# A static pipeline over heads in the gated-linear-attention stage

## The reference

```
cum = cumsum(log_a, within a chunk);  last = cum at the chunk's end
q_dec = q * exp(cum);  k_inv = k * exp(-cum);  k_end = k * exp(last - cum)
scores = tril(q_dec @ k_inv^T);  o_intra = scores @ v
upd = k_end^T @ v
S_next = exp(last) * S + upd;  o_inter = q_dec @ S
o = o_forward + flip(o_backward)
o = (o - mean(o)) * rsqrt(var(o) + 1e-5) * norm_g * silu(r)
```

## Time and profile before

| what | us |
|---|---|
| median of 3 runs (lowest, highest) | 3304.21 (3303.9, 3307.21) |
| the profiled execution's time | 3304.4 |
| its span, first to last instruction | 3302.6 |
| GLA stage, 528.4 to 1183.8 | 655.4 |
| of it PE busy, by the profile | 559.5 |
| one head | 157.2 |

### The profile page before, as it was taken

The page is one execution under the profiler, slowest core; times in us unless marked ns, Lnnn a source line. Parts: engine busy times, 40 slices in busy tenths (PEclk is TensorE's granted clock), DMA queues, the critical chain, the costliest instruction groups (busy, mean ns, idle before and its releaser), DMA issues. The chain is left out here.

```text
span 3302.6 us, 44198 instructions
## 1 busy us (share of the span) xinstructions
PE 2954.8 (89%) x17520; PEld 2849.0 (86%) x17520; DVE 1938.0 (59%) x2187; ACT 974.3 (29%) x1513; POOL 965.5 (29%) x458
## 2 busy tenths in 40 slices
PE   7999995979797959799996989999759999999993
PEld 7999995968686859799986989999649999999993
DVE  6666774253535376799996421455585555554556
ACT  2777774222313131244444110011240011100112
POOL 1121212111211012444541333434124333343430
PEclk9999997989898979899998999999879999999996
DMA  5132221010101033434334342322111111111111
GB/s 223 61 112 85 91 73 68 15 51 16 49 16 43 3 90 121 169 115 129 111 111 149 113 146 98 139 95 95 35 39 45 38 44 38 44 38 44 40 37 57
DMA packets 108091, 254.91 MB, mean 77 GB/s; under 512 B 20368, under 2 KB 51088, under 8 KB 107856
## 3 DMA queue, kind: packets, MB, share of 16 engines
q1 hardware_dynamic: 98192, 213.36, 19.4%
q10 hardware_dynamic: 9792, 40.11, 3.3%
HBM read 195.86 MB, written 57.55 MB: 77 GB/s over the span
## 5 line engine op out<-in xcount | busy, mean ns | idle before, releaser
L2063 PE MATMUL bank<-yhi,mrg_hi 128*128 128x384 f32 x1056 | 354.9, 336 | 34.3 <-POOL mrg_lo L167 20.6
L2063 PE MATMUL bank<-ylo,mrg_hi 128*128 128x384 f32 x1056 | 353.4, 335 | 0.0
L2063 PE MATMUL bank<-yhi,mrg_lo 128*128 128x384 f32 x1056 | 353.4, 335 | 0.0
L1417 PE MATMUL bank<-hhi,s_hi 128*128 128x384 f32 x768 | 265.6, 346 | 33.8 <-POOL s_lo L180 30.6
L164 POOL TENSOR_TENSOR mlp_hi<-mlp_raw,zero 128x1024 fp32r<-128x1024 f32 x64 | 121.9, 1905 | 534.5 <-PE bank L2390 225.9
L2390 PE MATMUL bank<-ahi,mlp_hi 128*128 128x384 f32 x768 | 257.4, 335 | 3.5 <-DVE alo L2439 3.5
L1417 PE MATMUL bank<-hhi,s_lo 128*128 128x384 f32 x768 | 259.4, 338 | 0.0
L1417 PE MATMUL bank<-hlo,s_hi 128*128 128x384 f32 x768 | 259.0, 337 | 0.0
L2390 PE MATMUL bank<-ahi,mlp_lo 128*128 128x384 f32 x768 | 256.6, 334 | 0.0
L2390 PE MATMUL bank<-alo,mlp_hi 128*128 128x384 f32 x768 | 256.5, 334 | 0.0
L2408 ACT ACTIVATE rl<-bank 128x384 f32<-128x384 f32 x96 | 47.0, 490 | 646.9 <-PE bank L2367 429.8
(11 more groups left out here) (396 smaller groups left out, 7758.4 us busy)
## 6 DMA issues: line engine op xcount, KB each, us to landing
mlp_raw<-in_mlp_units SPq DMA_DIRECT2D x64, 512.0 KB, 3.2
ada<-in_w_ada SPq DMA_DIRECT2D x32, 512.0 KB, 3.3
s_raw<-in_s_units SPq DMA_DIRECT2D x32, 512.0 KB, 4.3
mid_gates<-gate ACTq DMA_DIRECT2D x24, 576.0 KB, 3.5
gt<-mid_gates SPq DMA_DIRECT2D x24, 576.0 KB, 3.7
gla_raw<-in_gla_units SPq DMA_DIRECT2D x25, 512.0 KB, 3.6
lru_raw<-in_lru_units SPq DMA_DIRECT2D x24, 512.0 KB, 6.6
mid_s_tab<-tabq SPq DMA_DIRECT2D x8, 1152.0 KB, 7.6
```

The lines of the kernel that those rows point to most:

```text
L1417: mm = pe.matmul(out, wts[par][:, w], r[:, k, cols], start=(k == 0 and x == 0), stop=(k == KD - 1 and x == 2))
L2063: mm = pe.matmul(out, wt[par][:, w], r[:, slot, cols], start=(k == 0 and n == 0), stop=(k == len(order) - 1 and n == 2))
```

## The change

The `Fori` over heads is unrolled into a fixed order. While head h is in its 18 scan steps, PE also does one projection band in each step (v, q, k of head h+1 and r of head h-1, one band between scores(s+1) and outputs(s)) and small pieces of work called items: gates of this and the next head, transposes of the keys (three per item) and the mean and variance matmuls of head h-1. DVE and ACT get the matching work in the same step. Bands use banks 0 and 1, items banks 6 and 7, the scan banks 2 to 5, two for each step parity: scores with one update, and the other update with the output. `o` is doubled. r is no longer kept: each band goes to a buffer of 384 columns and is multiplied in at once. The root and the reciprocal are replaced by Ln and Exp with scale -0.5 on ACT. The high part of the weight split moves from POOL to ACT. On the host side only the order of the units in `gla_units` changes.

```diff
+        def step_band(h, s):
+            at = s if h else (s if s < 12 else None)
+            if h + 1 == HEADS:
+                at = s - 12 if s >= 12 else None
+            return [] if at is None else [HEAD_BANDS[h][at]]
+        def step_items(h, s):
+            got = []
+            if s == 0:
+                got.append(("gate", h, 1, 2))
+            if h and 1 <= s <= NB:
+                got.append(("mean", h - 1, 0, s - 1))
+            if h and 4 <= s < 4 + NB:
+                got.append(("var", h - 1, 0, s - 4))
+            if 7 <= s < 7 + NB:
+                got.append(("key", h, 1, s - 7))
+            if h + 1 < HEADS:
+                if s == 9:
+                    got += [("gate", h + 1, 0, 0), ("gate", h + 1, 0, 1)]
+                if s == 10:
+                    got.append(("gate", h + 1, 0, 2))
+                if s >= 15:
+                    got.append(("key", h + 1, 0, s - 15))
+            return got
+        def turn_items(h):
+            return [("value", h, 0, x) for x in range(NVT)] + [("gate", h, 1, 0), ("gate", h, 1, 1)]
...
-            return core.bank[3 * (s % 2) + 1 - c][:, P:P + DV]
+        def scores_psum(s):
+            return core.bank[2 + 2 * (s % 2)][:, 0:P]
+        def update_psum(s, c):
+            return core.bank[2 + 2 * (s % 2)][:, P:P + DV] if c else core.bank[3 + 2 * (s % 2)][:, 0:DV]
+        def out_psum(s):
+            return core.bank[3 + 2 * (s % 2)][:, DV:2 * DV]
...
+                def scores(h, s):                                   # PE
+                    g = NSTEP * h + s
+                    if g >= 2:
+                        pe.wait_ge(st_done, g - 1)
+                        pe.wait_ge(o_done, g - 1)
...
+                for h in range(HEADS):
+                    pe.wait_ge(band_free, 5 * NB if h == 0 else HEAD_BANDS[h - 1][2 * NB])
+                    for key in turn_items(h):
+                        item(key)
+                    scores(h, 0)
+                    for s in range(NSTEP):
+                        if s + 1 < NSTEP:
+                            scores(h, s + 1)
+                        for n in step_band(h, s):
+                            band(n)
+                        for key in step_items(h, s):
+                            item(key)
+                        outputs(h, s)
+                for x in range(NB):
+                    band(TAIL_BANDS[x])
+                    item(TAIL_MEANS[x])
+                band(TAIL_BANDS[NB])
+                for x in range(NB):
+                    item(TAIL_VARS[x])
+                for x in (4, 5):
+                    band(TAIL_BANDS[x])
...
+                    elif kind == "var":                             # ACT
+                        if NB * h + x:
+                            act.wait_ge(gm_done, NB * h + x)
+                        st(act.activation(scale[:], src[:, 0:BW], ACT.Ln, bias=eps[:, 0:1]))
+                        act.sem_inc(free_act, 1)
+                        act.activation(scale[:], scale[:], ACT.Exp, scale=-0.5).then_inc(rs_done, 1)
...
+                for h in range(HEADS):                              # DVE
+                    for s in range(NSTEP):
+                        advance(h, s)
                         if s:
-                            collect(s - 1)
+                            collect(h, s - 1)
+                        elif h:
+                            collect(h - 1, NSTEP - 1)
+                        if h >= 2 and s == 0:
+                            resonate(h - 2, 2 * NB - 1)
+                        if h and s <= NB:
+                            if s:
+                                centre(h - 1, s - 1)
+                            if s < NB:
+                                total(h - 1, s)
+                        if s == 5:
+                            keys(h, 1)
+                            queries(h, 1)
+                        if h and NB <= s < 2 * NB:
+                            spread(h - 1, s - NB)
+                        if h and 4 <= s < 4 + NB:
+                            normalise(h - 1, s - 4)
+                        if s == 2:
+                            forget(h, 1)
+                        if s == 3:
+                            accumulate(h, 1)
+                        if s == 6:
+                            ended(h, 1, 0)
+                            ended(h, 1, 1)
+                        if s == 7:
+                            ended(h, 1, 2)
...
+                        if h and s > 12:
+                            resonate(h - 1, s - 13)
```

More of the change, by code:

```diff
@@ L788, in start_state, with item_bank @@
+        counts = [0, 0]
+        for key in order + TAIL_MEANS + TAIL_VARS:
+            on_dve = key[0] == "mean"
+            ITEM[key] = len(FREED)
+            counts[on_dve] += 1
+            FREED.append((on_dve, counts[on_dve]))
+        def item_bank(key):
+            return core.bank[6 + ITEM[key] % 2]
         def start_state(s, c):
@@ L816, in _ @@
                 sync.dma_start(params[:], dram["gla_params"]).then_inc(small_in, 16)
+                load(1)
                 sync.dma_start(keep[:], dram["keep"]).then_inc(small_in, 16)
                 sync.dma_start(ident[:], dram["ident"]).then_inc(small_in, 16)
[L819 to L834, removed]
@@ L838, in _ @@
+                store_y(HEADS - 2)
+                store_y(HEADS - 1)
+                sync.wait_ge(y_out, 16 * HEADS)
                 for d in range(2):
-                    sync.wait_ge(final_out[d], 16 * HEADS + 16)
+                    sync.wait_ge(final_out[d], 16 * HEADS)
             @block.gpsimd
@@ L847, in _ @@
                         pool.memset(probs[d][s][:], 0.0).then_inc(const_done, 1)
[L848 to L852, removed]
+                for u in range(len(UNITS)):
+                    S.split_lo(pool, u, u % 2)
             @block.tensor
             def _(pe):
-                pe.wait_ge(const_done, 6)
@@ new lines, in band @@
+                def band(n):
+                    u, b = divmod(n, NB)
+                    if b == 0:
+                        pe.wait_ge(S.split_done, u + 3)
+                    if n >= 2:
+                        pe.wait_ge(band_free, n - 1)
+                    out = core.bank[n % 2][:, 0:BW]
+                    cols = slice(b * BW, (b + 1) * BW)
+                    for kk in range(KD):
+                        w = slice(kk * P, (kk + 1) * P)
+                        for x, (wts, r) in enumerate(((S.hi, hhi), (S.hi, hlo), (S.lo, hhi))):
+                            mm = pe.matmul(out, wts[u % 2][:, w], r[:, kk, cols],
+                                           start=(kk == 0 and x == 0), stop=(kk == KD - 1 and x == 2))
+                    mm.then_inc(band_mm, 1)
@@ L1106 @@
+                collect(HEADS - 1, NSTEP - 1)
+                resonate(HEADS - 2, 2 * NB - 1)
+                m = HEADS - 1
+                for b in range(NB):
+                    total(m, b)
+                    centre(m, b)
+                    if b:
+                        spread(m, b - 1)
+                spread(m, NB - 1)
+                for b in range(NB):
+                    normalise(m, b)
+                for x in range(2 * NB):
+                    resonate(m, x)
 G4 = 4
```

619 lines of the change are left out of this document (390 added, 229 removed).

## The result

The changed kernel took 3429.2 us (median of 4 runs, 3419.9 to 3431.0) against 3304.3 us for the kernel before on the same chip, a ratio of 1.037 (95% interval 1.035 to 1.039). The profiled execution has a span of 3428.6 us. From the GLA stage's first band (535.29, before 536.70) to S5's first band (1318.92, before 1195.50) it is 783.6 us against 658.8: 124.8 us more. So all of the loss is in this stage.

The account below looks back on a forecast made before the run. PE was taken as the bound, with 135 us over four heads idle or slow. Added idle of 182 us against that gave +47, the clock +28: 3304.4 + 75 = 3379 us, range 3312 to 3422.

Parts of the forecast that it names:

- rival A: The forecast's own case: added PE waits and falls of the clock slow the kernel to 3360 to 3400; chance 0.48.
- Waits of steps 1 to 6: Heads 1 to 3: PE held by the norm's mean (28 us, steps 1 to 3) and variance (50 us, steps 4 to 6).
- The trip: Each step: scores(s+1) waits for DVE to collect outputs(s-1), PE to DVE to PE; 0.74 us a step, 50 us.
- Table loads: Norm rounds and tail: ACT changes table for Ln and Exp, 1.28 us each; without these loads 31 us less, chance 0.08.
- Turn and tail: PE idle between heads, 13 us in all, and after the last head, 20 us.
- A fall thus costs half of 5.6 us: Heads 1 to 3, early steps: idle PE drops to half clock for 5.6 us; 28 us in all, at most 40.
- S: PE time of scores and updates in one scan step, taken as 0.72 us.
- Rival E: Low clock stays through most of steps 1 to 7, scans and norm products run longer; +114 us, 3418; chance 0.10.
- Rival B: Waits are there but the clock holds, PE being busy for more than half of each step; 3351; chance 0.20.
- The useful PE time of a head: Bands, scan steps, 384-column items and transposes of one head: 123.4 us of 157.2, the rest idle or slow.
- sum of added idle: Whole stage: trips, norm waits, turns, smaller waits, start and tail; 182 us against 135 given back, +47.
- Rival D: Norm hand-overs hidden, 50 us faster, 3254; decided by idle of steps 1 to 6, about 16 us a head; chance 0.14.

Follow-up runs that it names:

- e1: The changed kernel with scores(s+1) and its waits moved behind the band of the same step; 3301.7 us.
- e2: The changed kernel with the norm items one or two steps later against their producers and a second sum buffer, band's place unchanged; 3334.8 us.
- e3: The changed kernel with Identity in place of Ln in the variance steps, so ACT doesn't change its table there; 3404.5 us.
- e4: The kernel before with one wait added: scores(s+1) waits until step s-1's output has been collected; 3499.0 us.
- e9: The changed kernel with outputs of the 18 bandless steps in free projection banks, so scores(s+1) doesn't wait for the collect there; 3386.6 us.
- e5: The changed kernel with a spare band of 24 matmuls, result unused, in each of the 18 steps without a band; 3479.0 us.

## Why the prediction came out too low

The sign was right, and of rival A's mechanism these points:

- **Waits of steps 1 to 6**: 9.3 + 16.7 us a head beside the trips, 30.4 with them, measured 30.5, with errors of single steps that cancel (above). e1 and e2 show that this chain and its place are the cause: with either the place or the timing changed, the waits go.
- **The trip**: 0.56 to 0.61 us of idle PE in ordinary steps, against 0.74. Its effect on the clock wasn't priced at all (below).
- **Table loads**: as forecast, one of 1.28 us ahead of each of Ln and Exp in steps 5 and 6, and ahead of Exp alone in step 4. e3 gives 25 us for them against my 31. The Trainium skill ("ScalarE: Activation LUTs", section "Table sets: the hidden batching unit") has both functions in one set, so that the two need one load; the trace speaks against it here, with a load at 817.66 for Ln and another at 819.64 for Exp.
- **Turn and tail**: from head 1's value transposes to its scores it is 4.6 us (738.95 to 743.56), against my 4.8 for the seven items; the tail idles 14.19 us, near the 15 that I gave, and the matmuls behind it come every 0.32 us until 1294.24, at the low clock.

Two steps failed by being priced too low, and a third, priced too high, hid part of the error.

**"A fall thus costs half of 5.6 us ... in head 3, whose early steps have no bands, the half clock acts on S and the items only, 6 us."** This is the step that made the prediction too low. I took the time that a fall lasts from a stretch in which PE was busy throughout, and let every fall end after 5.6 us; heads 0 and 3 got 0 and 6 us. The traces show two other things. In heads 1 and 2 there are six falls each and not four, and they last 47.8 us together in head 1, not 4 x 5.6 = 22.4; each ends while the band behind it runs. By the ledger of e1 they cost 16.9 us and not 11. In steps without a band the low clock mostly stays: 84.5 us of head 3 ran at 0.58. An estimate of the whole: work that is done at 1.2 GHz would take half the time at 2.4, so a low stretch costs half of PE's busy time in it. The low stretches of the changed kernel's trace give 14, 16, 16 and 32 us for heads 0 to 3 and 3 for the tail, 81 us against the 28 that I had. e4 shows the low clock in scan steps without any pipeline over heads (a trip of 0.61 us, PE busy 90%, clock 0.50), and e9 from the other side (without the wait more of the steps run at 1.00, and head 3's early part gets 18.9 us of busy time back).

Rival E, at 3418, came nearest in number. Its mechanism, a clock that stays low through most of steps 1 to 7, is not what heads 1 and 2 show: their clock was 0.77 in these steps, low for less than half of the time, and e1 has the same bands at 1.00. Rival B, where the clock holds, is ruled out by the changed kernel's 0.87. PE's busy time was no reason to expect it to hold: e4's window has 0.50 with PE busy for 90%.

The trace of before held the hint: the scan that ran at 1.00 had next to no idle PE, 1.0 us of 43.4 in 18 steps. I used row 1707.2, 3.3 us of idle with the clock at 1.00, as the measure of what is harmless. It came once; a small gap that comes in each step is another case. The Trainium skill describes one like it, in "TensorE: Matmul & The Clock Gate", section "A second HAM failure mode: psum-queue depth-cycling": a kernel that cycles through PSUM banks leaves PE idle for moments between groups of matmuls, often enough that the clock oscillates. e4 agrees in that gaps of 0.61 us keep company with the low clock, and differs in that the clock stays at 0.50 through its window of 36 us. I had weighed only the section on oscillation ahead of it, on one long wait per tile.

**The useful PE time of a head.** I summed 123.4 us from pieces; e1's head 1 is busy for 131.5 us at full clock with the same matmuls. The 0.33 us behind the 64-row updates is the largest part (18 x 0.30 = 5.4 us: S is 1.02, not 0.72), and a band's first matmul holds PE 0.11 us longer than the others (884.95 to 885.23), 2 us more. The prediction's reading of the earlier trace rows was wrong there: the 0.33 us stands in a row of the weight loads, and PE was not waiting for the state. So I counted as given back what isn't.

Head 1 then adds up: predicted 123.4 + 11 clock + 43.6 idle (what is left of my 178) = 178, measured 131.5 + 16.9 + 39.0 = 187.4. Head 0 measured 130.9 against 115, head 3 137.5 against 120: together with 9.4 and 9.7 us of heads 1 and 2 that is 52 us, about all that the stage lost beyond the forecast. In heads 0 and 3 the clock (46 us against 6) is more than the 33 us by which they were too long.

**The idle time was priced too high.** The four heads idle 13.3, 39.0, 39.0 and 28.2 us and the tail 16.9, 136 us, where my sum of added idle was 182. In head 3 the norm's waits are shorter (at most 5.23 us, where head 1 has 6.70), and the trip was less than 0.74. Without this error the forecast would have missed by more; that it came as near as it did is luck in this part.

The break-even moves too. Rival D put it at 16 us of idle in steps 1 to 6. e1 has about a tenth of the changed kernel's idle in head 1 and only just ties with the kernel before, because the useful time is longer than I had and head 3 still stays at the low clock (granted clock 0.78 there).

What stays open: why the clock holds in e2's steps, with a trip and a band in each, and mostly not in e4's; and why e4's head 2 kept it for ten steps while head 0, with the same instructions and the same idle rows at its start, lost it at once. The runs show in which patterns it was kept, and not what decides. Nor was tried a version in which POOL's split keeps clear of the norm steps, or one in which every evacuation of the tail avoids the Silu load.

## What to carry to other kernels

When a static pipeline puts filler work between two dependent groups, put the filler ahead of the waiting instruction in the queue: moving one call behind the band was worth 127 us, and no operation changed. Price a small wait that comes back in each step at both levels of the clock, and not by its idle time alone: it made a 2.39 us step into 3.33 at the full clock and into 5.28 at the low one, and most of e4's steps ran at the low one. Take the useful time of an engine from a full-clock window of the same instructions, not from a sum of pieces, and don't count an idle row as a wait until you know whose row it is (matmuls or weight loads) and who ends it ("issue" names nobody).

## What the runs showed of the hardware

- Scan steps with a round trip over DVE (0.61 us of idle PE) ran at 1.2 GHz for long stretches (e4: 36.24 us at a granted 0.50, PE busy 32.59 us), and yet steps with the same wait ran at 2.4 GHz in head 2 of the same execution (29.88 us at 1.00, 0.76 us of idle PE each). Without the trip such steps ran partly at 2.4 GHz (e9: 1.00 in 4.79 us) and partly at 1.2 (717.60, 722.57). With a band of 24 matmuls in each step the clock was 1.00 in spite of the trip (e5: 41.42 us).
- The same idle stretches need not have the same effect. In e4's head 0 the first slow matmuls start at 645.33, behind idle stretches of 0.49 and 1.27 us at the start of the scan; head 2 has 0.50 and 1.28 us there (1054.86 and 1057.24) and kept 1.00 until after 1087.12. In the kernel before, 3.3 us ahead of 1710.5 didn't lower it.
- Behind four 64-row matmuls over 256 columns the weight loads pause for 0.33 us at the full clock and 0.65 us at the low one, whether the next group waits for a semaphore or not, while the matmuls' records run on (884.32 to 884.95 and 1199.65 above).
- A DVE add of 128x384 from SBUF took 2.52 us instead of 0.56 while POOL's split of 2.35 us ran (773.59 and 773.83 above). The cumulative sum took 4.66 us at 883.74, beside a split at 883.63, and 2.55 at 790.16 with none beside it.
